# A state-space layer's input product: from float32 on 32 array rows to stacked float32r parts that go through memory

## The reference, cut to what matters

```python
def s5_mixer(xin, lam_re, lam_im, log_dt, b_re, b_im, c_re, c_im, d, w_glu, b_glu):
    u = xin.astype(f32).reshape(bsz, seq, S5_GROUPS, S5_GROUP_CH)
    ...
    bu_re = jnp.einsum('blgh,gph->blgp', u, bb_re)
    bu_im = jnp.einsum('blgh,gph->blgp', u, bb_im)
    ...
    _, _, s_re, s_im = lax.associative_scan(combine, (a_re, a_im, bu_re, bu_im), axis=1)
    y = (jnp.einsum('blgp,ghp->blgh', s_re, c_re.astype(f32))
         - jnp.einsum('blgp,ghp->blgh', s_im, c_im.astype(f32)))
```

## Time and profile before

| | |
|---|---|
| median of three runs | 2958.08 us |
| the profiled execution | 2958.22 us |
| its span, first instruction to last | 2956.4 us |
| granted TensorE clock, mean | 1.0 |
| TensorE busy | 2944.8 us |
| VectorE, ScalarE, GpSimd busy | 1978.1, 1731.1, 441.8 us |
| DMA | 588.43 MB, mean 199 GB/s |

### The profile page before, as it was taken

How to read it: one execution, slowest core, us unless ns; L and a number is a source line. 1 busy time by engine, 2 the same in 40 slices (tenths; PEclk the granted TensorE clock), 3 DMA queues, 4 the chain that set the end, 5 groups by cost and what they waited for, 6 DMA issues and landing times.

```text
span 2956.4 us, 37411 instructions
## 1 busy us (share of the span) xinstructions
PE 2944.8 (100%) x13302; PEld 2427.1 (82%) x13302; DVE 1978.1 (67%) x2104; ACT 1731.1 (59%) x2454; POOL 441.8 (15%) x423
## 2 busy tenths in 40 slices
PE   9999999999999999999999999999999999999998
PEld 7888888888888888888887788888888888888887
DVE  6777754566667777676778886655556666666666
ACT  6876644547655555555675576554557554555555
POOL 1000110110035243320235450111000000000000
PEclk9999999999999999999999999999999999999999
DMA  8656666756666676676765555766656666666664
GB/s 259 185 157 199 199 200 194 200 182 200 192 192 221 191 225 198 214 222 190 262 193 197 195 186 168 219 206 209 206 202 186 199 192 195 193 192 192 192 192 163
DMA packets 298844, 588.43 MB, mean 199 GB/s; under 512 B 18464, under 2 KB 18480, under 8 KB 298352
## 3 DMA queue, kind: packets, MB, share of 16 engines
q1 hardware_dynamic: 292352, 563.61, 61.7%
q0 software_dynamic: 5952, 22.77, 2.5%
q10 hardware_dynamic: 432, 0.62, 0.1%
HBM read 574.35 MB, written 12.58 MB: 199 GB/s over the span
## 4 chain that ended last, share of the span: by engine, by line
PE 94%; DVE 2%; ACT 2%; issue 1%; DMA 1%; DVEq 0%; SPq 0%; ACTq 0%
PE banks L1733 94%; DMA raw<-in_w_in 1%; ACT whi L616 1%; DVE wlo L1117 1%; PE banks L1736 0%; ACT W L616 0%; ACT L616 0%; DVE W L1530 0%; DVE W L1522 0%; DVE banks L1523 0%; DVE banks L1525 0%; ACT G L616 0%; DMA Z<-in_x_t 0%; DVE W L1545 0%; DVE WR L1547 0%
## 5 line engine op out<-in xcount | busy, mean ns | idle before, releaser
L1117 DVE TENSOR_TENSOR wlo<-raw,whi 128x1024 fp32r<-128x1024 f32 x1047 | 1353.3, 1298 | 869.4 <-ACT whi L616 862.5
L616 ACT ACTIVATE whi<-raw 128x1024 fp32r<-128x1024 f32 (+1 forms) x1049 | 1105.9, 1059 | 1037.1 <-PE banks L1733 966.0
L1733 PE MATMUL banks<-whi,Y 128*128 128x512 f32 x4800 | 1484.6, 389 | 0.3 <-DVE W L1216 0.2
L1733 PEld LDWEIGHTS banks<-whi,Y 128*128 128x128 f32 x4800 | 901.1, 188 | 188.2 <-issue 0.9
L1733 PE MATMUL banks<-wlo,Y 128*128 128x512 f32 x2400 | 933.7, 389 | 0.0
L1733 PE MATMUL banks<-whi,XH 128*128 128x512 f32 x1792 | 705.2, 394 | 2.3 <-DVE wlo L1117 1.9
L1733 PE MATMUL banks<-whi,XL 128*128 128x512 f32 x1792 | 698.1, 390 | 0.0
L1733 PE MATMUL banks<-wlo,XH 128*128 128x512 f32 x1792 | 697.6, 389 | 0.0
L1733 PEld LDWEIGHTS banks<-wlo,Y 128*128 128x128 f32 x2400 | 450.6, 188 | 93.0
L1733 PEld LDWEIGHTS banks<-whi,XH 128*128 128x128 f32 x1792 | 336.5, 188 | 78.9 <-issue 7.9
L1733 PEld LDWEIGHTS banks<-whi,XL 128*128 128x128 f32 x1792 | 336.3, 188 | 71.2
(11 more groups left out here) (254 smaller groups left out, 1184.1 us busy)
## 6 DMA issues: line engine op xcount, KB each, us to landing
raw<-in_w_in SPq DMA_DIRECT2D x383, 512.0 KB, 3.9
raw<-in_w_mlp_up SPq DMA_DIRECT2D x128, 512.0 KB, 4.0
raw<-in_w_mlp_down SPq DMA_DIRECT2D x128, 512.0 KB, 3.9
raw<-in_w_mlp_in SPq DMA_DIRECT2D x128, 512.0 KB, 3.8
raw<-in_w_mlp_out SPq DMA_DIRECT2D x128, 512.0 KB, 3.7
raw<-in_w_branch SPq DMA_DIRECT2D x80, 512.0 KB, 4.2
raw<-in_w_out SPq DMA_DIRECT2D x64, 512.0 KB, 4.4
tables<-G POOLq DMA_DIRECT2D x8, 1024.0 KB, 8.2
```

Of the source, the lines that this page charges most:

```text
L616: return nc.scalar.activation(out_, in_, f, **kw)
L1117: tt(wlo[:, i % RING, :], raw[:, i % RING, :], whi[:, i % RING, :].bitcast(F32), ALU.subtract)\
L1733: return nc.tensor.matmul(out_, l, r, start=start, stop=stop, **kw)
```

## The change

B and the inputs are split into a float32r high part and a float32r rest, stored to memory, and read back as stacks of 128 rows. A stack of B has, from top to bottom, the high part of 32 rows twice, then its rest twice; a stack of inputs has the high part, the rest, the high part, the rest. One float32r matmul of 128 rows then gives all four products, where four float32 matmuls of 32 rows stood before there are four float32r ones of 128.

- GpSimd loads B as one transfer of 1 MB (`BRAW`) in place of two, with a layout made on the host; C's and the mask's loads share a semaphore.
- ScalarE copies B's two halves to `BHI` at positions 4 and 5 and the inputs' two halves to `UHI` at 21 and 29; VectorE subtracts, `BLO` at 6 and 7, `ULO` at 22 and 31.
- SP stores B's parts in four transfers of 512 KB at positions 12, 16, 20 and 24; ScalarE stores the inputs' parts in sixteen of 128 KB, four each at 22, 23, 33 and 35.
- ScalarE fetches stack 0 at position 25, stack 1 at 28 and stack m at 22 + 5m, into two alternating buffers: two transfers of 128 KB for B and one of 256 KB for the inputs, 2 KB per row. From m = 2 on it first waits for group m - 2 (`bu_mm`).
- TensorE's group 0 stands after unit 28 and not 26; every group waits for its stack.
- Semaphores are merged under new names (`scratch_saved`, `small2_in`, `gain_in`, `s5_hi`, `s5_lo`); their wait values are changed to match.

The diff, cut to its core:

```diff
-        BT = [slot(Z, 2 + r).rearrange("p (i c) -> p i c", i=8) for r in range(2)]
+        BRAW, BHI, BLO = slot(Z, 2, 2), slot(WR, 6, 2), slot(WR, 8, 2)
+        UIN, UHI, ULO = ([slot(t, i) for i in at] for t, at in ((W, (2, 3)), (WR, (4, 13)), (WR, (5, 5))))
+        SU = [slot(Y, 2)[:, CH * i:CH * i + CH].rearrange("p (e t) -> p e t", e=2) for i in range(2)]
+        SB = [slot(Y, 3)[:, CH * i:CH * i + CH].rearrange("p (r e s) -> p r e s", r=2, e=2) for i in range(2)]
...
+        SAVED = [64, 192, 320]
...
+            def s5_parts():
+
+                for n in range(4):
+                    yield 12 + 4 * n
+                    if n == 0:
+                        sp_.wait_ge(S("s5_lo"), 2)
+                    h, part = n // 2, n % 2
+                    sp_.dma_start(A["s5_b"][8 * h:8 * h + 8, part].rearrange("m (c x) n -> m c x n", x=4),
+                                  (BHI, BLO)[part][64 * h:64 * h + 64].bitcast(F32)).then_inc(S("s5_saved"), 16)
...
+                            stacks.upto(ch.u0 + i - u0[b, "a"])
...
+                pool.dma_start(BRAW, A["b_t"]).then_inc(S("s5_b_in"), 16)
                 for r in range(2):
-                    pool.dma_start(BT[r], A["b_t"][r]).then_inc(S("s5_b_in"), 16)
-                for r in range(2):
-                    pool.dma_start(CT[r], A["c_t"][r]).then_inc(S("s5_c_in"), 16)
-                pool.dma_start(GW, A["gm_w_t"]).then_inc(S("gm_w_in"), 16)
+                pool.dma_start(GW, A["gm_w_t"]).then_inc(S("small2_in"), 16)
...
+            def s5_stacks():
+                yield 25
+                act.wait_ge(S("s5_saved"), SAVED[1])
+                load_stack(0)
+                yield 28
+                load_stack(1)
+                for m in range(2, 16):
+                    yield S5Q + S5D * m - 4
+                    if m == 8:
+                        act.wait_ge(S("s5_saved"), SAVED[2])
+                    act.wait_ge(S("bu_mm"), 2 * m - 2)
+                    load_stack(m)
+
+            def load_stack(m):
+                for part in range(2):
+                    act.dma_start(slot(Y, 3)[64 * part:64 * part + 64, CH * (m % 2):CH * (m % 2) + CH].bitcast(F32),
+                                  A["s5_b"][m, part].unsqueeze(0).to_broadcast([2, 32, CH])).then_inc(S(f"s5_stack_in{m % 2}"), 16)
+                act.dma_start(slot(Y, 2)[:, CH * (m % 2):CH * (m % 2) + CH].bitcast(F32),
+                              A["s5_u"][m // 2, m % 2].rearrange("k c e t -> (k c) (e t)").unsqueeze(0).to_broadcast([2, 64, CH]))\
+                    .then_inc(S(f"s5_stack_in{m % 2}"), 16)
+
+            def save_inputs(h, part):
+                act.wait_ge(S(("s5_hi", "s5_lo")[part]), 3 + h)
+                m = (UHI, ULO)[part][h]
+                for c in range(4):
+                    act.dma_start(A["s5_u"][4 * h:4 * h + 4, c // 2, part, :, c % 2, :].rearrange("i c t -> c i t"),
+                                  m[32 * c:32 * c + 32].bitcast(F32).rearrange("p (i t) -> p i t", t=T))\
+                        .then_inc(S("s5_saved"), 16)
+
             def s5a():
 
+                for r in range(2):
+                    yield 4 + r
+                    act.wait_ge(S("s5_b_in"), 16)
+                    a(BHI[:, SL * r:SL * r + SL], BRAW[:, SL * r:SL * r + SL]).then_inc(S("s5_hi"), 1)
+                yield 21
+                act.wait_ge(S("stage_turned2"), 1)
+                a(UHI[0], UIN[0]).then_inc(S("s5_hi"), 1)
+                yield 22
+                save_inputs(0, 0)
+                yield 23
+                save_inputs(0, 1)
+                yield 29
+                act.wait_ge(S("stage_turned2"), 2)
+                act.wait_ge(S("c_scaled"), 1)
+                a(UHI[1], UIN[1]).then_inc(S("s5_hi"), 1)
+                act.wait_ge(S("s5_saved"), SAVED[1])
+                yield 33
+                save_inputs(1, 0)
+                yield 35
+                save_inputs(1, 1)
                 yield S5Q + 88
                 act.wait_ge(S("s5_y"), 8)
                 a(GS, GS, ACT.Gelu_apprx_tanh).then_inc(S("s5_g"), 1)
                 for h in range(2):
                     yield S5Q + 89 + h
                     act.wait_ge(S("s5_g"), 1)
-                    a(YH[:, 8 + 4 * h:12 + 4 * h, :], GS[:, 4 * h:4 * h + 4, :]).then_inc(S("s5_g_hi"), 1)
+                    a(YH[:, 8 + 4 * h:12 + 4 * h, :], GS[:, 4 * h:4 * h + 4, :]).then_inc(S("s5_hi"), 1)
...
-            def s5_g_lo():
+            def s5_lo():
+                for r in range(2):
+                    yield 6 + r
+                    dve.wait_ge(S("s5_hi"), 1 + r)
+                    c = slice(SL * r, SL * r + SL)
+                    tt(BLO[:, c], BRAW[:, c], BHI[:, c].bitcast(F32), ALU.subtract).then_inc(S("s5_lo"), 1)
+                for h in range(2):
+                    yield (22, 31)[h]
+                    dve.wait_ge(S("s5_hi"), 3 + h)
+                    tt(ULO[h], UIN[h], UHI[h].bitcast(F32), ALU.subtract).then_inc(S("s5_lo"), 1)
...
-                    yield S5Q + S5D * m
-                    i, c0 = m // 2, 64 * (m % 2)
-                    if m == 0:
-                        pe.wait_ge(S("s5_b_in"), 32)
-                        pe.wait_ge(S("stage_turned2"), 1)
-                    else:
-                        if m == 8:
-                            pe.wait_ge(S("stage_turned2"), 2)
+                    yield S5Q + S5D * m + (0 if m else 2)
+                    pe.wait_ge(S(f"s5_stack_in{m % 2}"), 48 * (m // 2 + 1))
+                    if m:
                         pe.wait_ge(S("s5_r_ready"), 2 * m)
                     for r in range(2):
                         for e in range(2):
-                            c = c0 + 32 * e
-                            ins = mm(PU[e][:, T * r:T * r + T], BT[r][c:c + 32, i, :], XI[c:c + 32, i, :],
-                                     tile_position=(c, 0))
+                            ins = mm(PU[e][:, T * r:T * r + T], SB[m % 2][:, r, e, :], SU[m % 2][:, e, :])
                     ins.then_inc(S("bu_mm"), 2)
...
-    m["b_t"], m["c_t"] = bt.reshape(2, P, 8, P), ct.reshape(2, P, 8, P)
+    m["b_t"] = bt.reshape(2, 2, 2, 32, 8, P).transpose(4, 1, 3, 0, 2, 5).reshape(P, 2 * SL)
...
+    aps["s5_b"] = nc.dram_tensor("s5_b", (16, 2, 32, CH), _mybir.dt.float32, kind="Internal").ap()
+    aps["s5_u"] = nc.dram_tensor("s5_u", (8, 2, 2, 32, 2, T), _mybir.dt.float32, kind="Internal").ap()
```

More of the change, by code:

```diff
@@ L383, in tables @@
                     if j == 0:
-                        sp_.wait_ge(S("tables_saved"), 32 * S5_TILES // TG)
+                        sp_.wait_ge(S("scratch_saved"), 32 * S5_TILES // TG)
                     if j >= NTAB:
@@ L401, in _ @@
                 branch = Steps(tables() if b == 2 else iter(()))
+                stacks = Steps(s5_parts() if b == 2 else iter(()))
                 for ph in "ab":
@@ L486, in block2 @@
                 pool.wait_ge(used, mlp_base(1, NF - 1))
+                pool.dma_start(BRAW, A["b_t"]).then_inc(S("s5_b_in"), 16)
                 for r in range(2):
-                    pool.dma_start(BT[r], A["b_t"][r]).then_inc(S("s5_b_in"), 16)
-                for r in range(2):
-                    pool.dma_start(CT[r], A["c_t"][r]).then_inc(S("s5_c_in"), 16)
-                pool.dma_start(GW, A["gm_w_t"]).then_inc(S("gm_w_in"), 16)
+                    pool.dma_start(CT[r], A["c_t"][r]).then_inc(S("small2_in"), 16)
+                pool.dma_start(GW, A["gm_w_t"]).then_inc(S("small2_in"), 16)
                 pool.wait_ge(evict["dve"], down0[1] + NF * NCH)
-                pool.dma_start(A["x1"].rearrange("(t p) n -> p t n", p=P), X).then_inc(S("x_saved"), 16)
-                pool.wait_ge(S("gm_w_in"), 16)
+                pool.dma_start(A["x1"].rearrange("(t p) n -> p t n", p=P), X).then_inc(S("scratch_saved"), 16)
+                pool.wait_ge(S("small2_in"), 48)
                 nc.gpsimd.affine_select(out=GW, in_=GW, compare_op=ALU.is_ge, fill=0.0, base=0,
@@ L503, in block2 @@
                 kr, ki, nkr = (k.unsqueeze(2).to_broadcast([P, 32, 32]) for k in (D_KR, D_KI, D_NKR))
-                pool.wait_ge(S("s5_c_in"), 32)
                 pool.wait_ge(S("s5_factors"), 1)
@@ L529, in block2 @@
                         if j == 24:
-                            pool.dma_start(GMG, A["gm_norm_g_2"][0].partition_broadcast(P)).then_inc(S("gm_gain_in"), 16)
+                            pool.dma_start(GMG, A["gm_norm_g_2"][0].partition_broadcast(P)).then_inc(S("gain_in"), 16)
                         else:
@@ L543, in make_tables @@
                     if g:
-                        pool.wait_ge(S("tables_saved"), 32 * g)
+                        pool.wait_ge(S("scratch_saved"), 32 * g)
                     nc.gpsimd.memset(c[:, :, 0:1], 1.0)
@@ L562, in make_tables @@
                         pool.dma_start(A["tables"][TG * g:TG * g + TG, :, i, :].rearrange("j p t -> p j t"), m)\
-                            .then_inc(S("tables_saved"), 16)
```

(27 more changed lines are left out.)

2 lines of the change are left out of this document (1 added, 1 removed).

## The result

The changed kernel takes 3019.9 us (median of four runs, 3016.8 to 3021.1) against 2958.07: 61.8 us slower, ratio 1.0207, 95% interval [1.0189, 1.0225]. The forecast was +41 us, in a range of 2953 to 3040 us.

What follows compares the result with a forecast made beforehand. TensorE, with 94% of the chain, was taken as the bound. Two loaded DMA engines make group 15 42 us late, hiding the other terms; less its own 0.6 saving, 2958.2 + 41 = 2999 us, range 2953 to 3040.

Steps and rivals of the forecast that it cites:

- The stack loads: Sixteen 512 KB stacks on ScalarE's queue: last lands at 1791.5, group 15 comes 42 us late, +41 us net.
- two shares: Leading count of 2 puts each stack on two DMA engines: 7.37 MB at 24.9 GB/s, 296 us; chance 0.73.
- By halves: The two-engine sum split at group 9: 4.54 MB, 34 us late; then 2.82 MB, 8 us more.
- The weights starve too: Rival: weight transfers share the two engines by turns, a few us per group at most, up to 3040; within the 0.73.
- The 1.2 GHz level: TensorE's clock falling after stack waits: up to about 4 us per group stay hidden behind the next stack.
- The product: TensorE's state-space groups: four float32r matmuls take 0.68 us, not 1.29; saves 0.61 a group, 9.8 over 16.
- First group two units later: Group 0 after unit 28: low parts of units 30 and 31 late, TensorE waits 2.0 + 1.9 = 3.9 us.
- Splits and stores at zero: ScalarE's copies, VectorE's subtractions and the stores cost zero; issues zero until the attention stage.
- no stall: The wait for the stored parts comes about two units after the first half's last store, so costs nothing.
- sixteen shares: Stacks divided over all 16 engines, 32 KB per engine and stack: nothing waits; chance 0.15.
- the first two rivals: Stacks over all engines, attention stage taking back 2.2 us: 2954.5 (0.15); the same with ScalarE's issues counting: 2961 (0.06).

Runs made afterwards that it cites:

- e1: The changed kernel with each stack fetched in six transfers, one per copy, instead of three: 2960.05 us.
- e8: The changed kernel with four transfers per stack instead of three, 32 rows outermost, B's repeat inside the transfer: 2957.2 us.
- e11: e10 with eight transfers of 32 rows per stack, dealt as 4 outermost and 8 inside, no repeated source: 2957.75 us.
- e2: The changed kernel with only B's stacks in one transfer per copy; the inputs' transfer keeps its repeated source: 2970.3 us.
- e12: e10 with eight transfers per stack, 32 rows outermost, no repeated source; the control for e11: 2950.4 us.
- e3: The changed kernel with stacks 2 to 15 fetched to a scratch in memory, nobody waiting; all products read stacks 0 and 1: 3017.95 us.
- e5: e1 with TensorE's group 0 back after unit 26: 2957.45 us.
- e7: e1 with the edits of both e5 and e6: 2953.0 us.
- e10: e7 with e8's four transfers per stack, and stacks 0 and 1 also issued by SyncE after position 29: 2950.5 us.
- e6: e1 with stacks 2 to 15 issued by SyncE between the weight loads instead of by ScalarE: 2955.35 us.

## Why the prediction came out so

**The stack loads.** Right in mechanism: two shares (96 closing packets; e1, e8, e11), stacks of 14 to 23 us each, and a stream that is still going when group 15 is due: its last packet ends at 1811.4, 1.2 us before that group. Mis-sized: the term gave +41 us, and the kernel lost 61.8. Of its inputs, the start was 1495.5 and came out as 1498.5, because ScalarE waited for the stores. The speed was taken as 24.9 GB/s. From 1498 to 1794, when group 14 got its stack, the two engines carried 15 x 0.262 = 3.93 MB of stacks and a sixteenth of the rest, (189 x 296 us = 55.9 MB, less 15 x 0.524) / 16 = 3.0 MB: 6.93 MB in 296 us, 23.4 GB/s. With 23.4 and 1498.5 the prediction's own 7.37 MB end at 1813.5, and group 15 ran at 1812.6. So the burst rate was 6% too high for this mix of stack rows and weights: 7.37 MB take 315 us and not 296, which with the 3 us at the start is all that was missing. The 23.4 is read back from the result, so this places the error and doesn't prove it. By halves: +34 was forecast to group 9 and +8 more after it; group 9 ran 49.7 us late and group 15 13.6 more. The prediction's 4.54 MB to group 9, at 23.4 GB/s from 1498.5, end at 1692.5, and the last packet of stack 9 ended at 1692.8: the same speed fits both halves.

The sum by average doesn't give every loss: 5.28 MB on the hottest engines needs 212 us of 255 (226 at 23.4 GB/s), and e2 and e11, which have just that, lose 10.3 and 7.4 us where it gives none. Keeping up on the average still leaves short queues: e11's waits for the low part are 6.5 us, e12's 2.1.

**"The weights starve too"** was put as a rival that adds a few us per group. It isn't an addition: e3, with the same time, speaks for the same bound seen from the other side. The 1.2 GHz level behind long waits, which the prediction thought hidden, came too (14.3 us inside the units, 14.2 in e3); the sum of bytes with 23.4 GB/s leaves no room for it as a separate term.

**The product.** Taken as 0.68 us, with 0.45 as the lower bound; measured at the lower bound. The timeline of PE in e1 between units 46 and 47:

```profile
1569.83 0.39 PE L1806 MATMUL banks<-whi,XL 128*128 128x512 f32 x1
1570.05 0.64 PE L1806 MATMUL banks<-Y 128*128 128x256 f32 x4
1570.53 0.40 PE L1806 MATMUL banks<-whi,XH 128*128 128x512 f32 x1
```

0.70 us between two weight matmuls, less one plain step: 0.47. A group that stands alone saves 0.79 us (by the starts of units 46 and 51), one with an output group 0.55 to 0.6, not 0.61 each.

**First group two units later.** Predicted 3.9 us, as waits of 2.0 and 1.9. In e1 the step into unit 30 is 2.2 us too long and unit 30 itself 1.8, 4.0 in all. The size held, the shape didn't: TensorE waited 2.0 us for unit 30, ran it at 1.2 GHz, and so waited only 0.1 us for unit 31, whose low part was ready at 1522.8 either way. e5 still loses 1.1 us there, so moving the group got 2.6.

**Splits and stores at zero** held up to unit 25: every kernel starts it within 0.8 us of the kernel before. But "no stall" at the wait for the stored parts was wrong: in e5 ScalarE's copy of unit 26 started after 3.5 us of idleness, in e7 after 4.6 and in the changed kernel after 3.5. In e10, where ScalarE doesn't wait there, units 30 and 31 are on time. With two shares the stores were not free either: one of them held the sequencer 9.27 us.

**Rivals.** With sixteen shares the first two rivals bracket the truth: 2954.5 and 2961 forecast, 2960.05 measured. Issues do count; six per stack cost 4.7 us (e6), where 6.7 was forecast for three. About 2 of the 4.7 us stand for the slow clock at one unit. The attention stage's chain is there too: e10 keeps 8.1 of the 8.5 us that it has at unit 82 and nothing of the four groups behind it.

**Open.** In the changed kernel the clock's share can't be told apart from the waits ahead of it. Why issues hold ScalarE's sequencer for 4 to 9 us is not shown: the backlog alone isn't the reason, as e3's issues of few large packets into the same two engines took 0.60 us at most. No run has two shares with SyncE as the issuer. Whether the two engines were always the same pair was not seen engine by engine; the sum takes it so, and e3's time agrees.

## What to carry to other kernels

Look at the outermost count of every DMA before its bytes: a stack that is fetched as "two copies of a block" belongs in one transfer per copy, or with the repeat inside (60 of 62 us here). The mean DMA share hides it; count closing packets, and compare the landings of *other* transfers (the weights' went from 4.7 to 9.4 us). When a shared DMA engine is full, removing the wait you see can only move it to the next user (e3), so change the load and not the wait. And put small issues on the queue of the engine that has slack: the same fetches cost 4.7 us more on ScalarE than on SyncE, and on SyncE twice the number cost nothing (e12).

## What the runs showed of the hardware

- An outermost count of 2 closes with 2 packets per transfer (the changed kernel), of 4 with 4 (e11), of 32 or more with 16 (e1, e12); a repeat inside changes nothing (e8).
- Two engines with both streams gave about 23.4 GB/s each over 296 us; bursts over all 16 gave 24.9 and 27.3. The Trainium skill's figure ("DMA: Bandwidth & Descriptors", "Specifications"), about 27 GiB/s, is above all three; the measurements decide.
- A DMA issue on ScalarE took 0.31 to 1.26 us in e1 and up to 9.27 us in the changed kernel, with two DMA engines full; the engine's next copy waited behind it. Issues from memory to memory in packets of 64 KB took 0.53 to 0.60 us with the same two full (e3).
- Waits of 4.5 to 7.2 us are followed by TensorE steps of 0.43 us in place of 0.23 for about half a unit to a whole one; one of 2.0 us (e1, unit 30) was too. One of 1.56 us (the changed kernel, 1528.3) and four of 0.65 to 0.81 us in e10 were not.
- Four 128-row float32r matmuls of 256 columns cost 0.47 us together, 0.02 more than two of 512 columns (e1).
